# Both output projections of a two-layer decoder trunk: the third row group of their last two column blocks as a seven-product group

## What is computed

```python
x = x + diff_attention(rms_norm(x)) ; x = x + sq_relu_mlp(rms_norm(x))     # layer 0
... # shared latent keys and values
x = x + mla_attention(rms_norm(x))  ; x = x + sq_relu_mlp(rms_norm(x))     # layer 1
return rms_norm(x)

def diff_attention(...):  ...; return o.reshape(B, S, 2048) @ w_o
def mla_attention(...):   ...; return o.reshape(B, S, 2048) @ w_o
def sq_relu_mlp(h, w_up, w_down):  return jnp.square(jax.nn.relu(h @ w_up)) @ w_down
```

## Time and profile before

| | us |
|---|---|
| median of 3 runs (lowest, highest) | 1980.34 (1980.28, 1980.65) |
| the profiled execution | 1980.67 |
| its span, first to last instruction | 1977.9 |
| TensorE busy | 1968.6 |
| VectorE busy | 1649.0 |
| ScalarE busy | 1221.1 |
| mean granted clock of TensorE, share of full speed | 0.999 |

### The profile page before, as it was taken

One profiled execution on the slowest core, in us unless ns is written; L12 is line 12 of the kernel. 1 busy time (PEld: TensorE's weight loads), 2 busy tenths in 40 slices (PEclk: granted clock), 3 DMA queues, 4 the chain that ended last, 5 costly groups with the idle time before them and its releaser, 6 DMA issues.

```text
span 1977.9 us, 24520 instructions
## 1 busy us (share of the span) xinstructions
PE 1968.6 (100%) x9080; PEld 1641.7 (83%) x9080; DVE 1649.0 (83%) x2015; ACT 1221.1 (62%) x1563; POOL 34.4 (2%) x45
## 2 busy tenths in 40 slices
PE   9999999999999999999999999999999999999998
PEld 7888888888888888888888998888888888888887
DVE  7789996678988998898886787667998898898886
ACT  6555555557667566656656665556566666666663
POOL 0000000000000000000000000000000000000000
PEclk9999999999999999999999999999999999999999
DMA  8655546766787587677666554676587678658663
GB/s 306 214 171 188 175 167 204 225 199 216 224 243 232 189 243 234 218 231 225 224 213 213 146 152 143 229 222 223 194 231 234 224 228 241 207 205 256 216 233 118
DMA packets 269405, 418.23 MB, mean 211 GB/s; under 512 B 18800, under 2 KB 88816, under 8 KB 269296
## 3 DMA queue, kind: packets, MB, share of 16 engines
q1 hardware_dynamic: 254096, 396.87, 61.1%
q0 software_dynamic: 3456, 12.58, 3.4%
q10 hardware_dynamic: 11744, 7.34, 1.3%
HBM read 379.00 MB, written 2.10 MB: 193 GB/s over the span
## 4 chain that ended last, share of the span: by engine, by line
PE 97%; issue 2%; DVE 0%; ACT 0%; POOL 0%; POOLq 0%; DVEq 0%; ACTq 0%
PE acc L617 23%; PE acc L619 23%; PE acc L618 23%; PE side L852 3%; PE side L853 3%; PE side L851 3%; PE acc L851 2%; PE acc L853 2%; PE acc L852 2%; PE acc L637 2%; PE acc L638 2%; PE acc L639 2%; PE acc L966 1%; PE acc L967 1%; PE acc L968 1%
## 5 line engine op out<-in xcount | busy, mean ns | idle before, releaser
L1745 DVE TENSOR_TENSOR wlo<-raw,whi 128x1024 fp32r<-128x1024 f32 (+2 forms) x564 | 669.5, 1204 | 141.5 <-ACT whi L1113 139.9
L1113 ACT ACTIVATE whi<-raw 128x1024 fp32r<-128x1024 f32 (+2 forms) x564 | 579.2, 1046 | 331.1 <-PE acc L619 264.3
L617 PE MATMUL acc<-whi,opA 128*128 128x512 f32 (+2 forms) x1072 | 414.7, 387 | 0.0
L619 PE MATMUL acc<-whi,opA 128*128 128x512 f32 (+2 forms) x1072 | 413.9, 386 | 0.0
L618 PE MATMUL acc<-wlo,opA 128*128 128x512 f32 (+2 forms) x1072 | 413.8, 386 | 0.0
L617 PE MATMUL acc<-whi,opB 128*128 128x512 f32 x976 | 381.1, 390 | 0.0
L619 PE MATMUL acc<-whi,opB 128*128 128x512 f32 x976 | 380.0, 389 | 0.0
L618 PE MATMUL acc<-wlo,opB 128*128 128x512 f32 x976 | 379.8, 389 | 0.0
L619 PEld LDWEIGHTS acc<-whi,opA 128*128 128x128 f32 x1072 | 201.3, 188 | 40.2
L617 PEld LDWEIGHTS acc<-whi,opA 128*128 128x128 f32 x1072 | 201.3, 188 | 40.0
L618 PEld LDWEIGHTS acc<-wlo,opA 128*128 128x128 f32 x1072 | 201.3, 188 | 40.0
(11 more groups left out here) (382 smaller groups left out, 2733.9 us busy)
## 6 DMA issues: line engine op xcount, KB each, us to landing
raw<-in_w_up SPq DMA_DIRECT2D x128, 1024.0 KB, 5.9
raw<-in_w_down SPq DMA_DIRECT2D x128, 1024.0 KB, 5.1
raw<-in_a_w_qkv SPq DMA_DIRECT2D x44, 1024.0 KB, 5.1
prob<-o_sb SPq DMA_DIRECT2D x136, 128.0 KB, 2.6
raw<-in_a_w_o SPq DMA_DIRECT2D x16, 1024.0 KB, 5.1
raw<-in_b_w_o SPq DMA_DIRECT2D x16, 1024.0 KB, 5.1
raw<-in_w_ukv SPq DMA_DIRECT2D x32, 256.0 KB, 4.2
xs<-junk POOLq DMA_DIRECT2D x12, 512.0 KB, 5.3
```

Of the source, the lines that this page charges most:

```text
L617: mm(o, a_hi, w_hi, start=start, stop=False)
L619: done = mm(o, a_lo, w_hi, start=False, stop=last and c == chunks - 1)
L1113: done = fn(whi[:, place:place + ch, 0:n], raw[:, r, c0:c0 + ch, 0:n], ACT.Copy)
L1745: done = tt_(wlo[:, place:place + ch, 0:n], raw[:, r, c0:c0 + ch, 0:n], whi[:, place:place + ch, 0:n].bitcast(F32), ALU.subtract)
```

## The change

Both `out_proj` change in the same way. Blocks 1 and 2 stay. Of blocks 3 and 4 the rows of the third quad (chunks 8 to 11) are worked off together as one group of seven products. TensorE's order is: halves 0 to 3 of block 3, the group, the last two halves of block 3, then six halves of block 4 (chunks 0 to 7, 12 to 15). SP loads the quads in the order (3rd block: 0, 1, 2; 4th: 2; 3rd: 3; 4th: 0, 1, 3). The activation forms are made in block 2. VectorE adds the combined share to the stream itself. The chunks of x are turned later: chunk 3 after the share, between halves 6 and 7 of block 4's list. `combine`, `form_sums`, `form_low`, `low` and the three `seven` are moved out of `mlp` unchanged; counters (`FORM_SETS`, `GROUP`, `SHARE`) grow by the new group.

```diff
-    made = [("up", l, 0, 1)]
+    made = [("out", l), ("up", l, 0, 1)]
-FORM_SETS = 2 + 2 * (QUARTERS - 1)
+FORM_SETS = 3 + 2 * (QUARTERS - 1)
...
@@ sync @@
-            with sp.Fori(0, JB) as j:
-                whole(B_WO + j, W_O, NB * j)
+            def out_proj(b0, w):
+                with sp.Fori(0, 2) as j:
+                    whole(b0 + j, w, NB * j)
+                for i, (j, r) in enumerate(((2, 0), (2, 1), (2, 2), (3, 2), (2, 3), (3, 0), (3, 1), (3, 3))):
+                    quad(b0 + 2 + i // 4, i % 4, w[:, 4 * r:4 * r + 4, NB * j:NB * j + NB], later=int(i == 6))
...
@@ tensor @@
-                for j in range(1, JB):
-                    s = (j + 1) % 2
-                    block_tok(b0 + j, s, uses[s] + j // 2, opB)
+            def out_proj(l, b0, uses):
+                block_tok(b0 + 1, 0, uses[0], opB)
+                b = b0 + 2
+                for hf in range(4):
+                    half_tok(b, hf, 1, chunks_of(opB, 2 * hf), first=hf == 0, uses=uses[1] + 1)
+                shares_free(SHARE["out", l])
+                pe.wait_ge(form_lo, FORM_SETS * l + 1)
+                seven(GROUP["out", l], b, 4, opB, 8, [forms[0][:, i] for i in range(2)], uses[0] + 1, True, SHARED)
+                for hf in range(2):
+                    half_tok(b + 1, hf, 1, chunks_of(opB, 12 + 2 * hf), last=hf == 1)
+                for hf in range(2, 8):
+                    half_tok(b + 1, hf, 0, chunks_of(opB, 2 * hf - 4 if hf < 6 else 2 * hf), first=hf == 2, last=hf == 7,
+                             uses=uses[0] + 1, starts=(False, True))
...
@@ scalar @@
                 x_squares(v0, 1, uses[1] + 1)
-                for j in range(1, JB):
-                    s = (j + 1) % 2
-                    body(b0 + j, {4: lambda: x_move(v0 + j - 1), 7: lambda: x_hi(v0 + j - 1, gain)})
-                    x_squares(v0 + j, s, uses[s] + j // 2 + 1)
+                body(b0 + 1, {4: lambda: x_move(v0), 6: lambda: form_high(forms[0][:, 0], FORM_SETS * l),
+                              7: lambda: x_hi(v0, gain)})
+                x_squares(v0 + 1, 0, uses[0] + 1)
+                b = b0 + 2
+                split(b, 3)
+                x_move(v0 + 1)
+                seven(GROUP["out", l], b, 4, (2, b), (3, b), {"T4": lambda: x_hi(v0 + 1, gain)})
+                for hf in range(4):
+                    split(b + 1, hf)
+                act.wait_ge(xsq, 2 * (v0 + 2))
+                copy_shared()
+                for hf in range(4, 8):
+                    split(b + 1, hf)
+                act.wait_ge(out_added, 2 * l + 2)
+                x_squares(v0 + 2, 1, uses[1] + 2)
+                split(b + 2, 0)
+                x_move(v0 + 2)
+                split(b + 2, 1)
+                split(b + 2, 2)
+                x_hi(v0 + 2, gain)
+                x_squares(v0 + 3, 0, uses[0] + 2)
...
@@ vector @@
                 add_product(b0, 1, uses[1], slice(0, NB))
                 x_turn(v0, 1, 2 * (uses[1] + 1))
-                for j in range(1, JB):
-                    s = (j + 1) % 2
-                    body(b0 + j, {7: lambda: x_lo(v0 + j - 1, gain)})
-                    add_product(b0 + j, s, uses[s] + j // 2, slice(NB * j, NB * j + NB))
-                    x_turn(v0 + j, s, 2 * (uses[s] + j // 2 + 1))
+                body(b0 + 1, {4: out_form_sums, 7: lambda: x_lo(v0, gain),
+                              8: lambda: form_low(down_form(0), FORM_SETS * l)})
+                add_product(b0 + 1, 0, uses[0], slice(NB, 2 * NB))
+                x_turn(v0 + 1, 0, 2 * (uses[0] + 1))
+                b = b0 + 2
+                seven(GROUP["out", l], b, 4, (2, b), (3, b), 8 * b + 3,
+                      {"first sum": lambda: split(b, 3), "T4": lambda: x_lo(v0 + 1, gain)})
+                for hf in range(4):
+                    split(b + 1, hf)
+                combine(SHARE["out", l], down_shared)
+                split(b + 1, 4)
+                dve.wait_ge(pe_halves, 8 * b + 10)
+                add_product(None, 1, uses[1] + 1, slice(2 * NB, 3 * NB))
+                split(b + 1, 5)
+                dve.wait_ge(drained[1], 2 * (uses[1] + 2))
+                share_added()
+                split(b + 1, 6)
+                dve.wait_ge(out_added, 2 * l + 2)
+                x_turn(v0 + 2, 1, 2 * (uses[1] + 2))
+                split(b + 1, 7)
+                split(b + 2, 0)
+                split(b + 2, 1)
+                split(b + 2, 2)
+                x_lo(v0 + 2, gain)
+                add_product(b + 1, 0, uses[0] + 1, slice(3 * NB, 4 * NB))
+                x_turn(v0 + 3, 0, 2 * (uses[0] + 2))

```

More of the change, by code:

```diff
@@ L799, in last_block @@
+            out_proj(0, B_WO, U_WO)
             def last_block(b, s, uses, other_uses):
@@ L824, in mlp @@
                 u = U_MLP[l]
[L826 to L859, removed]
                 def pair(q, uses):
@@ L1407, in square_second @@
                     square()
[L1409 to L1412 removed]
                 def down_forms(q, g):
[L1415 to L1419, removed]
+                    form_high(forms[g][:, 0], FORM_SETS * l + 2 * q + g + 2)
                 def scale_shared(key):
@@ L1426, in scale_shared @@
                         fn(both, both, ACT.Copy, scale=rs[:, 2 * l + 1, t:t + 1]).then_inc(shared_scaled, 1)
[L1428 to L1446, removed]
-                            hf = hf0 + IN_RING.index(f)
-                            act.wait_ge(pe_halves, 8 * b + hf - 3)
-                            fn(whi[:, 2 * (hf % 4):2 * (hf % 4) + 2, :], source[f], ACT.Copy).then_inc(hi_ready, 1)
-                        if f in between:
-                            between[f]()
                 def first_down(q):
@@ new lines, in seven @@
+            def seven(group, b, hf0, own, other, lows_before, after):
+                (o, o_loads), (t, t_loads) = own, other
+                n, e = 4 * group, 3 * group
+                b11, b21 = raw[:, o, 0:2, :], raw[:, o, 2:4, :]
+                b12, b22 = raw[:, t, 0:2, :], raw[:, t, 2:4, :]
+                dve.wait_ge(raw_ready[o], 16 * o_loads + 16)
+                dve.wait_ge(raw_ready[t], 16 * t_loads + 16)
+                dve.wait_ge(lo_ready, lows_before)
+                tt_(w_sum, b11, b12, ALU.add).then_inc(w_summed, 1)
+                after["first sum"]()
+                dve.wait_ge(w_summed, n + 1)
+                tt_(b12, b12, b22, ALU.add).then_inc(w_summed, 1)
+                if "second sum" in after:
+                    after["second sum"]()
+                low("B22", group, b, hf0, b22)
+                low("T1", group, b, hf0, w_sum)
+                dve.wait_ge(w_summed, n + 2)
+                dve.wait_ge(lo_ready, 8 * b + hf0 + 1)
+                tt_(b22, w_sum, b22, ALU.add).then_inc(w_summed, 1)
+                low("B21", group, b, hf0, b21)
+                dve.wait_ge(w_summed, n + 3)
+                dve.wait_ge(extra_lo_ready, e + 1)
+                tt_(w_sum, b22, b21, ALU.add).then_inc(w_summed, 1)
+                low("B11", group, b, hf0, b11)
+                if "B11" in after:
+                    after["B11"]()
+                low("T2", group, b, hf0, b22)
+                if "T2" in after:
+                    after["T2"]()
+                low("T3", group, b, hf0, b12)
+                dve.wait_ge(w_summed, n + 4)
+                low("T4", group, b, hf0, w_sum)
+                if "T4" in after:
+                    after["T4"]()
@@ new lines, in down_form, with out_proj, out_form_sums, share_added @@
+            def down_form(g):
+                return [forms[g][:, i] for i in range(2)]
+            def out_proj(l, b0, uses, v0, gain):
+                def out_form_sums():
+                    tt_(act_whole, opB[:, 8:12, 0, :].bitcast(F32), opB[:, 8:12, 1, :].bitcast(F32),
+                        ALU.add).then_inc(act_rebuilt, 1)
+                    dve.wait_ge(act_rebuilt, 2 * l + 1)
+                    form_sums(act_whole.rearrange("p f (a n) -> p f a n", n=32), FORM_SETS * l)
+                def share_added():
+                    dve.wait_ge(shared_sums, 4 * SHARE["out", l] + 4)
+                    for t, both in enumerate((junk[:].rearrange("p a n -> p (a n)"), o_sb[:].rearrange("p a t n -> p (a t n)"))):
+                        tt_(xs[:, t, 2 * NB:4 * NB], both, xs[:, t, 2 * NB:4 * NB], ALU.add).then_inc(out_added, 1)
```

207 lines of the change are left out of this document (115 added, 92 removed).

## The result

The changed kernel takes **1988.53 us** (median of 6 runs, 1985.38 to 1990.85) against 1980.47 (1979.70 to 1981.27, 6 runs) for the kernel before, run beside it on the same chip: ratio 1.0041, 95% interval [1.0029, 1.0052], **8.1 us slower**. Slower was forecast, 5.0 us; the measured median lies 0.7 us above the top of the range. The profiled execution took 1987.58 us, with a span of 1985.8: 7.9 us over the span before.

A forecast was written before the change was run, and what follows sets the result against it. TensorE was taken as the bound, with other engines hidden. Removed matmuls (-2.3 us) and pauses (+7.3) summed to +5.0 us, from the median 1980.34 to 1985.3 us; range 1979.9 to 1987.8.

The forecast's parts named there:

- What bounds the kernel: Whole kernel: TensorE busy 1968.6 of 1977.9 us, so the gain is at most the matmuls removed.
- TensorE: Both projections: 48 matmuls (10.88 us) replaced by a 9.74 us group, 1.14 us less each, 2.3 us in both.
- VectorE in amount: Per projection: 16.8 us of added VectorE work fits in 21.6 us idle over three blocks; amount does not stall it.
- Block 2 and the group: Projection blocks 2 and 3: block 2 unchanged, group without stall, tightest form ready 350.8, wanted 351.2; then a 0.2 us pause.
- rival 3: Inside the group: one VectorE operation slips and stalls it, +2.3 us in both projections, 1987.6 us; chance 0.06.
- The pause before block 4: Before half 0 of block 4: its low part ready at 356.95, wanted at 356.75, a pause of 0.2 us.
- Block 4 and what is queued behind it: Block 4 hidden but chunk 3's move issued at 372.15, not 361.80; MLP pauses 1.6 us before half 3, 2.4 before half 6.
- The rule M3 + M4 - 16.0: Each projection's shift in us, from the DMA move times of x chunks 3 and 4 (M3, M4): +3.0 and +2.0.
- Which M: Move times of chunks 3 and 4: 9.4 + 9.6 us in projection 1, 9.5 + 8.5 in projection 2; bounds 7.9 and 9.6.
- Rival 4: Pauses let TensorE's clock fall to 1.2 GHz, 2.72 us per slow half; one per projection gives 1990.7 us; chance 0.02.
- rival 1: Moves of chunks 3 and 4 land early, 7.9 to 8.8 us each: 1980.0 to 1983.5 us; chance 0.27.
- Rival 2: No load runs beside the moves of chunks 3 and 4, or they need no wait: 1978.4 us; chance 0.05.

The follow-up runs named there:

- repeat: The changed kernel run again unchanged, timed beside the kernel before: 1987.86 us, ratio 1.0036.
- the filled one: Changed kernel plus matmuls nobody reads, five and sixteen, ahead of TensorE's waits for MLP halves 3 and 6: 1985.60 us, ratio 1.0027 against the kernel before.
- the order experiment: Changed kernel with chunk 4's squares, addition and transposition queued before chunk 3's high and low parts, loads unchanged: 1980.97 us, ratio 1.0004 against the kernel before.
- the control: The kernel before, with SP's weight loads held back during the move of chunk 4 only: 1980.66 us, ratio 1.0003.

## Why the prediction was wrong, point by point

**What bounds the kernel, TensorE, VectorE in amount: right.** The 12 matmuls per kernel are gone, and with the loads held back the time falls by 2.5 us [0.8 to 4.4 by the interval] where 2.3 was summed. VectorE's 31 us more cost nothing in that kernel.

**Block 2 and the group: right, one term 0.2 us too high.** Nothing stalls inside the group; rival 3 is out. The pause before block 4 is not there: the 0.25 us between a low part's end and its matmul was too much.

**Block 4 and what is queued behind it: right in place and mechanism.** The pauses stand before half 3 and half 6 of the MLP's first block, in both projections. The rule M3 + M4 - 16.0 gives with the measured moves 18.35 - 16.0 = +2.4 for projection 1 (the trace: +2.1) and 19.5 - 16.0 = +3.5 for projection 2 (+3.2); both are 0.2 to 0.3 too high. Of that 0.15 is the 0.2 us allowed between the last low part and the matmul (0.05 in the trace, 398.84 to 398.89), and some 0.1 the issue of move 3, which came that much sooner. Undoing either half of the mechanism, the loads beside the moves or the order of the queues, takes away 10 or 7 us.

**Which M: wrong for one of four.** I took 8.5 us for the last move of projection 2 because the last move had that in the kernel before; it took 10.1, 9.6 and 9.5 us in three profiles of this order (changed kernel, its repeat, the filled one). The four moves' sum was taken at 37.0 and measured 37.86 (changed kernel) and 37.7 (repeat): the two shifts came to 5.3 us instead of 5.0, the moves 0.9 longer and the rule 0.5 too high in both projections together. The upper bound, 9.6, was too low as well: 10.1, and 10.3 in the order experiment. I had the bound from eight moves only, and took their lengths without asking which load they followed: in the trace of the kernel before, too, the last piece of moves 3 and 4 lands 0.4 to 0.5 us after the load issued 1.2 us into the move, which took 6.8 to 7.9 us.

**Rival 4: the step that failed.** The sum had no term for the clock, and the range left it out. The rival had 0.02, "my pauses are at most 2.4", against the last 8 us of the kernel, in which the clock had stayed high for about half the stretch. But that row gives a mean over the kernel's end; no row of before has a pause of this size with matmuls behind it (its longest wait is 1.1 us). Measured: after pauses of 2.8 us (changed kernel), 2.7 (order) and at most 2.2 (repeat) the clock was at 1.2 GHz; after one of 2.0 in the changed kernel it was not. The low level began with the first matmul behind the pause (order), the third (changed kernel) or the sixth and seventh (repeat), so in the changed kernel and its repeat TensorE was at work again when the clock fell. One fall costs 1.6 us rather than the 2.72 that the rival charged for a whole half at the low level, as TensorE was back at 2.4 GHz after some eight slow matmuls. By the mean clock it came in nine of the eleven runs of the changed kernel; two of these have a trace. The forecast's 5.0 plus 2.3 to 2.7 of clock is 7.3 to 7.7, against the measured 7.6 (repeat) and 8.1.

**Rivals 1 and 2.** No move of the changed kernel took under 8.9 us, so rival 1 is out. Rival 2's world, no load beside the moves, was built: it forecast 1978.4 and measured 1977.7.

The range should have reached higher: a case "late moves and one or two falls of the clock" is the forecast's 1985.3 plus 1.6 to 3.2 us, 1986.9 to 1988.5, and with the forecast's own upper bound, 1986.7, up to 1989.9.

What stays open: why the load that a move's last piece follows takes 6.4 us in one execution or place and 8.1 in another, so that the move takes 8.2 or 10.3, and why the clock fell after pauses of up to 2.2 us in one execution and held after 2.0 in another. No run here tells.

## What to carry to other kernels

A piece of work that an engine hands to a DMA and then awaits in order makes the DMA's latency part of that engine's queue: before moving such work later, ask which operations stand behind the wait, and what big transfers run beside it. Put the operations that feed the next DMA ahead of the wait, and issue the small DMAs in the queue of the big loads, or hold these back: here the one turned 8 us lost into 1 us lost, which the measurement does not tell from none, the others into 2 us gained. When a sum of pauses of 2 to 3 us on TensorE comes out, add the clock: price one fall as a case of its own.

## What the runs showed of the hardware

- A 128 KB piece lands in 2.6 to 3.3 us (once 3.6) when the 1 MB loads are held back or stand behind it in the same queue, and in up to 8.1 us (changed kernel) or 8.3 (order) when they run beside it from another queue; the last piece of a move then lands 0.3 to 1.0 us after the load issued 1.1 to 1.2 us into the move. The Trainium skill (DMA: Bandwidth & Descriptors, Queues, rings and completion order) says that each engine serves all queue rows with work in turn; the trace agrees in that the same piece in the loads' own row was not slowed.
- TensorE's clock went to 1.2 GHz after pauses of 2.2 to 2.8 us, once with no other pause in that projection, and stayed there for seven to nine matmuls (0.63 us each, 0.43 apart): 1.5 to 1.6 us each time. With five and sixteen small matmuls in the pauses the mean clock was 0.999 in all nine runs, and the one trace shows no fall.
- Held loads cost nothing that the measurement sees (the control: 1.0003 [0.9993, 1.0012]), and behind the held loads TensorE waited for no weight.
